# Gated linear attention on one core: a head's level 0 operands taken in a step of their own, its output products put inside the last projection

## The reference

```python
def step(s, blk):
    qc, lfc, kc, vc = blk
    b = jnp.cumsum(lfc, axis=2)
    decay = jnp.exp(jnp.where(lower, b[:, :, :, None, :] - b[:, :, None, :, :], -jnp.inf))
    a = jnp.einsum('bhtd,bhsd,bhtsd->bhts', qc, kc, decay)
    o = jnp.einsum('bhts,bhse->bhte', a, vc) + jnp.einsum('bhtd,bhde->bhte', qc * jnp.exp(b), s)
    b_last = b[:, :, -1:, :]
    s_new = jnp.exp(b_last)[:, :, 0, :, None] * s + jnp.einsum('bhsd,bhse->bhde', kc * jnp.exp(b_last - b), vc)
    return s_new, o
...
    ol_f, _ = hgrn_direction(ql_h, to_heads(pl[1], HG_DK), il_h, lb_fwd, sc_f, False)
    ol_b, _ = hgrn_direction(ql_h, to_heads(pl[2], HG_DK), il_h, lb_bwd, sc_b, True)
    a_lat = hgrn_readout(ol_f + ol_b, pl[4], hg_norm_g)
```

## Time and profile before

| | |
|---|---|
| median of three runs | 2934.95 us |
| the profiled execution | 2931.62 us |
| its span, first to last instruction | 2929.8 us |
| mean granted TensorE clock | 0.982 of full |
| PE busy | 2781.7 us (95%) |
| DVE busy | 1107.5 us (38%) |
| ACT busy | 512.8 us (18%) |
| DMA, mean over the span | 127 GB/s |

### The profile page before, as it was taken

How to read it: one execution, slowest core, us unless ns; L and a number is a source line. 1 busy time by engine, 2 the same in 40 slices (tenths; PEclk the granted TensorE clock), 3 DMA queues, 4 the chain that set the end, 5 groups by cost and what they waited for, 6 DMA issues and landing times.

```text
span 2929.8 us, 29804 instructions
## 1 busy us (share of the span) xinstructions
PE 2781.7 (95%) x11878; PEld 1652.7 (56%) x11878; DVE 1107.5 (38%) x2115; ACT 512.8 (18%) x883; POOL 0.2 (0%) x4
## 2 busy tenths in 40 slices
PE   7999999999899999999699999989989998999997
PEld 3566556666644444444343343324378696888886
DVE  3134443333444443401401111135355244654654
ACT  1111111121132332311100000022322103100001
POOL 0000000000000000000000000000000000000000
PEclk9999999999999999999899999999999999999999
DMA  8621111110111111122599999962200431333331
GB/s 310 225 58 43 57 50 50 43 43 29 29 37 46 54 51 44 51 72 72 209 359 409 409 409 409 409 224 58 58 1 18 139 103 29 87 87 87 89 90 38
DMA packets 326948, 372.41 MB, mean 127 GB/s; under 512 B 9953, under 2 KB 272822, under 8 KB 323510
## 3 DMA queue, kind: packets, MB, share of 16 engines
q1 hardware_dynamic: 326208, 369.72, 36.7%
q10 hardware_dynamic: 630, 1.16, 0.1%
HBM read 368.75 MB, written 2.10 MB: 127 GB/s over the span
## 4 chain that ended last, share of the span: by engine, by line
PE 91%; DVE 3%; DVEq 2%; ACT 1%; issue 1%; DMA 1%; ACTq 0%; SPq 0%
PE psum L1351 17%; PE psum L613 14%; PE psum L1651 12%; PE psum L1185 8%; PE psum L1739 6%; PE psum L1286 4%; PE psum L604 3%; PE psum L925 2%; PE psum L1544 2%; PE psum L684 2%; PE psum L1320 2%; PE psum L2260 2%; PE psum L1577 2%; PE psum L1115 2%; PE psum L1164 1%; PE psum L1144 1%
## 5 line engine op out<-in xcount | busy, mean ns | idle before, releaser
L1351 PE MATMUL psum<-arena 128*128 128x256 f32 x2240 | 484.5, 378 | 0.5 <-ACT arena L2358 0.5
L613 PE MATMUL psum<-arena 128*128 128x512 f32 (+1 forms) x1152 | 460.9, 553 | 2.9 <-DVE arena L511 2.9
L1351 PEld LDWEIGHTS psum<-arena 128*128 128x128 f32 x2240 | 422.7, 189 | 61.9 <-ACT arena L2358 0.7
L1651 PE MATMUL psum<-arena 128*64 128x512 f32 x1536 | 347.6, 597 | 3.0 <-issue 2.1
L613 PEld LDWEIGHTS psum<-arena 128*128 128x128 f32 x1152 | 216.4, 192 | 211.8 <-issue 204.5
L1185 PE MATMUL psum<-arena 128*128 128x512 f32 x512 | 233.1, 597 | 0.0
L1651 PEld LDWEIGHTS psum<-arena 128*64 128x64 f32 x1536 | 104.9, 136 | 217.5 <-issue 214.4
L1739 PE MATMUL psum<-arena 128*128 128x512 f32 (+1 forms) x448 | 167.6, 532 | 0.0
L1185 PEld LDWEIGHTS psum<-arena 128*128 128x128 f32 x512 | 92.3, 189 | 104.1 <-issue 104.1
L1582 DVE SCALAR_TENSOR_TENSOR arena<-psum,arena 128x512 f32<-128x512 f32 x64 | 48.0, 750 | 246.7 <-PE psum L1577 246.2
L1739 PEld LDWEIGHTS psum<-arena 128*128 128x128 f32 x448 | 85.1, 190 | 82.2 <-issue 78.8
(11 more groups left out here) (335 smaller groups left out, 2982.1 us busy)
## 6 DMA issues: line engine op xcount, KB each, us to landing
arena<-in_w_gate SPq DMA_DIRECT2D x64, 1024.0 KB, 18.4
arena<-in_w_up SPq DMA_DIRECT2D x64, 1024.0 KB, 16.2
arena<-in_w_down SPq DMA_DIRECT2D x64, 1024.0 KB, 17.9
arena<-in_w_in SPq DMA_DIRECT2D x120, 512.0 KB, 3.8
arena<-in_ada_w SPq DMA_DIRECT2D x24, 1024.0 KB, 7.8
arena<-in_w_up SPq DMA_DIRECT2D x32, 512.0 KB, 5.4
arena<-in_w_down SPq DMA_DIRECT2D x32, 512.0 KB, 4.8
arena<-in_w_out SPq DMA_DIRECT2D x16, 512.0 KB, 3.7
```

The lines of the kernel that those rows point to most:

```text
L613: mm = pe.matmul(bank[:, 0:b - a], w[:, k, :], HT[:, k, a:b], start=(k == 0), stop=(k == KC - 1))
L1351: mm = pe.matmul(psum[:, base + b, c * HALF:(c + 1) * HALF], w, v, start=(first and q == 0 and m in (0, 2, 3, 4)), stop=(last and q == KC ...
L1651: mm = pe.matmul(psum[64 * e:64 * e + 64, bank + n, :], tokens(e, 2 * q + k), w[:, k, 512 * n:512 * n + 512], start=(q == 0 and k == 0), s ...
```

## The change

Two of the eight instructions of `dve_take`, those that make `hw_q0` and `hw_k0`, become a step of their own, `dve_begin`, with a drain and a semaphore `head_begun`. It stands in front of `dve_readout` of the head before (and once before the loop). Level 0 waits for `head_begun` in place of `head_taken`. ScalarE's waits for `head_taken` stay. The waits on the pieces move with the new step.

The 12 output products no longer follow piece 10 but stand inside it, between its sixth and its seventh matmul. The norm's matmul stays behind the piece. In the tail, where the eighth head's outputs have no piece around them, they are as before.

```diff
-        def pe_piece(pe, i, j):
+        def pe_piece(pe, i, j, within=None):
...
                     if k == 0:
                         first(mm)
+                    if within is not None and k == KC - 3:
+                        within()
             mm.then_inc(sem(f"piece_{j % 2}"), 1)
...
             if l == 0:
-                pe.wait_ge(sem("head_taken"), i)
+                pe.wait_ge(sem("head_begun"), i)
...
-        def dve_take(dve, i):
+        def dve_begin(dve, i):
 
             dve.wait_ge(sem("piece_out_0"), i * 6)
             dve.wait_ge(sem("piece_out_1"), i * 5)
+            dve.tensor_copy(hw_q0, hp_q)
+            dve.tensor_tensor(hw_k0, hp_k[:, 0, C:T], hp_k[:, 1, C:T], ALU.add)
+            dve.drain()
+            dve.sem_inc(sem("head_begun"), 1)
+
+        def dve_take(dve, i):
+
             dve.tensor_tensor(hw_q[:, 1, :], hp_q, hp_f[:, 0, C:T], ALU.mult)
             dve.tensor_tensor(hw_q[:, 0, :], hp_q, hp_f[:, 1, C:T], ALU.mult)
-            dve.tensor_copy(hw_q0, hp_q)
-            dve.tensor_tensor(hw_k0, hp_k[:, 0, C:T], hp_k[:, 1, C:T], ALU.add)
             dve.tensor_copy(hw_k, hp_k)
...
                 for j in range(len(PIECES)):
-                    pe_piece(pe, i, j)
+                    pe_piece(pe, i, j, (lambda: pe_outputs(pe, i)) if j == 10 else None)
...
                     if j == 10:
-                        pe_outputs(pe, i)
                         pe_head_norm(pe, i)
...
             dve_mod_late(dve)
+            dve_begin(dve, 1)
             with dve.Fori(1, HEADS) as i:
                 dve_take(dve, i)
...
                 dve_states(dve, i)
+                dve_begin(dve, i + 1)
                 dve_readout(dve, i)
```

## The result

| | before | changed |
|---|---|---|
| median of four runs | 2933.61 us | 2906.97 us (2905.78 to 2912.56) |
| ratio to before | | 0.992, interval 0.9908 to 0.9932 |
| profiled execution | 2931.62 us | 2905.78 us |
| span | 2929.8 us | 2904.0 us |
| PE busy | 2781.7 us | 2772.2 us |

The change makes the kernel 26.6 us faster. Forecast were 2904 us, with 2897 to 2911 as the bounds that cover most and a reach to 2914. All medians are of fast runs: of the eight runs of the kernel before in the last group of experiments, two took 3321 and 6972 us at a granted clock of 0.84 and 0.385, and are left out.

What follows compares the result with a forecast made beforehand. TensorE was taken to bound the kernel (91% of the chain). 13.0 - 0.7 + 6.8 + 9.7 = 28.8 us off 2931.62 gave 2902.8, with half of 3.3 us added 2904 us; 2897 to 2911 covers most, reach to 2914.

Steps and rivals of the forecast that it cites:

- Level 0's wait in the loop: TensorE before level 0, six passes: the wait for the take goes, 2.17 us each, 13.0 us gained.
- The outputs inside piece 10: End of each pass: norm 0.1 us later, ScalarE's square behind the query's copy; seven passes +0.7 us, from -2.8 to +4.2.
- The clock in the loop: TensorE in the loop: no clock fall behind the norm's gap of about 1.3 us; 4 x 1.70 = 6.8 us back.
- The tail: Eighth head: level 0 directly behind the norm, new 1.4 us wait before level 1; 9.7 us gained, bounds 7.5 to 11.
- I let the whole shift pass to the end: Behind the tail: waits are only for work TensorE has fed, never a transfer, so the whole shift reaches the end.
- Half of the 3.3 us to the median: Whole kernel: half the 3.3 us between profiled execution and median added to 2902.8 us, giving 2904 us.
- The clock does keep falling: Rival, gap before the norm: the clock still falls, 6.8 us not gained or more lost; 2911 to 2916 us; chance 0.10.
- The tail gave its share: Rival, tail: readout and take on VectorE are the true bound, only 3 us come through; 2911 us; chance 0.06.
- No wait for a transfer: Rival, later stages: a wait for a transfer keeping its own time loses all the gain; 2931 to 2935 us; chance 0.04.
- The slower one: Rival, inside piece 10: outputs wait for states coming 6.6 us later than now, beyond 1.7 us cover; 2938 us; chance 0.02.

Runs made afterwards that it cites:

- The filled gap: Two more 128x512 matmuls, results unread, between piece 0 and level 0 of every pass, against the kernel before: 2926.87 us, ratio 0.9983.

## Why the prediction was right

- **Level 0's wait in the loop: right.** Six gaps of 2.17 us were taken to go, and went. With the step alone a pass takes 81.76 us in place of 84.0, so 2.25 each: level 0 itself is 0.1 us shorter without the gap. The step ended 2 us before the readout, as worked out.
- **The outputs inside piece 10: right.** Taken at +0.1 us a pass, measured 0.10 (81.87 less 81.76). The kernel with the outputs alone shows the same, 84.09 us in place of 84.0. The reason given, ScalarE's order, was shown by turning it round: 1.06 us a pass back, where 7 us in seven passes had been named. That ScalarE's queue is strictly first in, first out is what the Trainium skill states in "TensorE: Matmul & The Clock Gate", section "Architectural detail"; the traces agree, with L784 at 216.18 us, 2.2 us after its input was ready and behind L646 at 215.68.
- **The clock in the loop: right.** 6.8 us were taken for four falls, and 6.7 measured. The clock never falls behind the new gap of 1.2 us, in seven passes of each of five traces that have it. Passes, norm to norm, went from 84.0 and 85.7 to 81.87 us: 6 x 2.25 - 6 x 0.10 + 6.7 = 19.6, measured 19.5. The filled gap shows that the gap of 2 us was the cause. That the clock bears one of 1.2 us had been inferred from shorter gaps before; these five traces are what shows it.
- **The tail: right, a size off by 0.35 us.** 9.7 us were taken, 9.35 measured. Level 1 lasts 1.4 us until the next instruction starts, not 0.9, as it had done at 748.33 already. The new wait is 1.3 us by the prediction's way of counting, from the end of issue (1.15 in the bracket), not 1.4.
- **"I let the whole shift pass to the end": this step was mis-sized.** 30.4 us arrive at the end of the tail of the first trace, 1.5 of them luck ahead of the loop, and 25.84 at its end. That no wait takes up the shift holds: no single wait there grew by more than 0.3 us. But the clock took it, at the three places named above, where the changed kernel's trace has half clock under running matmuls and the first trace of before has not. The loss came in all three traces of the changed kernel. The forecast had 3 us each way for it and nothing in its middle. Without the luck and the loss the profiled execution would have been near the 2902.8 us worked out; with both it was 2905.78.
- **Half of the 3.3 us to the median: no mechanism stood behind it.** The later medians of before are 2932.0 to 2932.3 us, hardly above the 2931.62 of the profiled execution. What these 1.2 us added happened to lie on the side of the loss: 2904 us were forecast and 2907.0 measured, and by medians the gain is 25.6 to 26.6 us where 28.8 was the sum.
- **The rivals.** The clock does keep falling, but not where the rival put it: not behind the norm's gap, but in the tail and behind it. The tail gave its share but for 0.35 us. No wait for a transfer is among TensorE's waits later. The slower one was out of reach by 1.7 us of cover (the states end at 209.36 us, the outputs start at 211.08), and is real when the cover is taken.

## What to carry to other kernels

A step that copies a set of buffers for the next round can be cut at what the waiting engine needs first; where that part stands only matters where the wait has no other cover, which here was one place of eight, and worth 6.5 us. Before products are moved into another group to hide a wait, look at the order of the engine that must answer: here the moved outputs cost 0.1 us a pass until the square was put ahead of the copy, and gave 0.95 with it. And count a short wait of TensorE with the clock that may fall behind it, and half clock only where matmuls run in it and no later wait takes it up.

## What was not expected of the hardware

A wait of 2.0 us before level 0 costs 1.7 us more in four cases of six, in each of three traces, and two useless matmuls in each such wait win back 5.3 us of a kernel. And the 2100 us behind the tail, unchanged in code, take 2099.5 to 2110.4 us, within 1.1 us for the same kernel (three traces of the changed one, two of before): at the places looked at, the same matmuls behind the same wait run at full clock in one kernel's trace and at half in another's.
